# The MLP of the first joint layer as seven products of quarter blocks over 768 tokens, and one block for the compression weights

## The reference

```python
def sq_relu_mlp(h, w1, w2):
    return jnp.square(jax.nn.relu(h @ w1)) @ w2
...
        x = x + ml[5] * sq_relu_mlp(modulate(rms_norm_2(x, norm2_g[i]), ml[3], ml[4]), mlp_w1[i], mlp_w2[i])
        if ctx_later:
            h_ctx = h_ctx + mc[2] * yc
            h_ctx = h_ctx + mc[5] * sq_relu_mlp(modulate(rms_norm_2(h_ctx, norm2_g[i]), mc[3], mc[4]),
                                                mlp_w1[i], mlp_w2[i])
```

## Time and profile before

| | us |
|---|---|
| median of 3 runs | 4087.72 (4080.39 to 4090.18) |
| profiled execution | 4087.81 |
| its span, first to last instruction | 4085.7 |
| PE busy | 3926.6 (96%) |
| DVE busy | 1751.1 (43%) |
| ACT busy | 932.8 (23%) |
| POOL busy | 506.3 (12%) |
| mean granted TensorE clock | 0.978 |

### The profile page before, as it was taken

One profiled execution on the slowest core, in us unless ns is written; L12 is line 12 of the kernel. 1 busy time (PEld: TensorE's weight loads), 2 busy tenths in 40 slices (PEclk: granted clock), 3 DMA queues, 4 the chain that ended last, 5 costly groups with the idle time before them and its releaser, 6 DMA issues.

```text
span 4085.7 us, 42004 instructions
## 1 busy us (share of the span) xinstructions
PE 3926.6 (96%) x16600; PEld 2671.4 (65%) x16604; DVE 1751.1 (43%) x3123; ACT 932.8 (23%) x2131; POOL 506.3 (12%) x414
## 2 busy tenths in 40 slices
PE   9999979999999999999999899999999999999997
PEld 4458436545655565656545578888558888678886
DVE  2654444732673223111010555654675665224343
ACT  1141213621452211100010442020312111212020
POOL 1000000000000000000000421112432121111121
PEclk8999989999999999999999999999999999999999
DMA  3112332021002123223121314443202444112221
GB/s 125 62 42 84 116 98 79 1 74 41 24 1 61 62 82 107 100 99 108 62 72 64 86 30 154 165 167 103 83 21 83 165 165 144 67 62 83 83 83 42
DMA packets 226770, 342.38 MB, mean 84 GB/s; under 512 B 32209, under 2 KB 100209, under 8 KB 226545
## 3 DMA queue, kind: packets, MB, share of 16 engines
q1 hardware_dynamic: 202064, 322.44, 23.0%
q0 software_dynamic: 6816, 10.01, 1.2%
q10 hardware_dynamic: 17696, 7.26, 0.7%
HBM read 334.01 MB, written 4.06 MB: 83 GB/s over the span
## 4 chain that ended last, share of the span: by engine, by line
PE 73%; DVE 3%; POOL 1%; ACT 1%; issue 1%; DMA 0%; DVEq 0%; ACTq 0%; POOLq 0%
PE psum L1638 28%; PE psum L1407 28%; PE psum L1591 5%; PE psum L1595 3%; PE psum L1762 2%; PE psum L1709 2%; PE psum L1739 1%; PE psum L1507 1%; POOL arena L2774 1%; PE psum L1367 1%; DVE small L2594 1%; ACT arena L2079 1%; DVE psum L2590 0%; DVE arena L2609 0%; PE psum L1665 0%
## 5 line engine op out<-in xcount | busy, mean ns | idle before, releaser
L1407 PE MATMUL psum<-H,ring 128*128 128x512 f32 (+1 forms) x3248 | 1160.5, 517 | 38.1 <-DMA ring<-in_cd_in 22.8
L1407 PEld LDWEIGHTS psum<-H,ring 128*128 128x128 f32 x3248 | 622.0, 193 | 554.8 <-issue 483.9
L1638 PE MATMUL psum<-arena,ring 128*128 128x256 f32 x1536 | 342.8, 380 | 2.8 <-ACT arena L1876 2.8
L2296 DVE SCALAR_TENSOR_TENSOR arena<-ring,cond,arena 128x512 f32<-128x512 f32 x448 | 320.5, 754 | 8.0
L1638 PEld LDWEIGHTS psum<-arena,ring 128*128 128x128 f32 x1536 | 290.4, 190 | 44.0 <-ACT arena L1876 5.3
L2731 POOL TENSOR_TENSOR ring<-ring 128x1024 f32<-128x1024 f32 x48 | 159.6, 3325 | 791.0 <-DVE arena L2143 791.0
L1638 PE MATMUL psum<-arena 128*128 128x256 f32 x1152 | 256.3, 379 | 0.4
L1638 PEld LDWEIGHTS psum<-arena 128*128 128x128 f32 x1152 | 218.6, 190 | 30.3 <-ACT arena L1881 0.7
L2594 DVE TENSOR_REDUCE small<-psum 128x1 f32<-128x512 f32 (+7 forms) x352 | 187.0, 566 | 116.8 <-PE psum L1721 51.6
L2279 DVE TENSOR_TENSOR mods<-psum,vec 128x4 f32<-128x4 f32 (+1 forms) x48 | 7.7, 161 | 509.1 <-PE psum L1367 508.2
L1591 PE MATMUL psum<-arena,ring 128*128 128x512 f32 x512 | 225.6, 593 | 0.2 <-issue 0.2
(11 more groups left out here) (230 smaller groups left out, 4612.2 us busy)
## 6 DMA issues: line engine op xcount, KB each, us to landing
ring<-in_mlp_w SPq DMA_DIRECT2D x64, 2048.0 KB, 8.8
ring<-in_ada_w SPq DMA_DIRECT2D x48, 2048.0 KB, 7.9
ring<-in_na_qkv SPq DMA_DIRECT2D x6, 2048.0 KB, 8.0
ring<-in_ab_in SPq DMA_DIRECT2D x5, 2048.0 KB, 8.2
ring<-in_cd_in SPq DMA_DIRECT2D x4, 2048.0 KB, 7.7
ring<-in_pw SPq DMA_DIRECT2D x8, 1024.0 KB, 6.8
ring<-in_at_qkv SPq DMA_DIRECT2D x3, 2048.0 KB, 7.8
ring<-in_ab_out SPq DMA_DIRECT2D x2, 2048.0 KB, 8.2
```

What stands on the lines that cost most here:

```text
L1407: last = nc.tensor.matmul(out, lhs, rhs, start=(k == 0), stop=(k == len(t.pairs) - 1))
L1638: last = nc.tensor.matmul(bank(at, HALF, HALF * m), w[:, i, P * m:P * m + P], x[:, i, :], start=(opens and m == 0 and i == 0), stop=(i == ...
L2296: ins = nc.vector.scalar_tensor_tensor(partial[:, v, :], w[:, k, :], cond[:, k, v:v + 1], partial[:, v, :], ALU.mult, ALU.add)
```

## The change

**The joint MLP** (`joint_mlp` takes the place of `mlp_ctx`) becomes a fast stage. The normed x and context are written side by side into one tensor, `J`, of 8 tiles x 768 columns, which takes the place of `H` and `CH`. The inner layer is made in four quarters of 1024 rows. A quarter is four units up and four down. A unit is seven products, each four matmuls deep over 384 columns, for two output tiles of 128 rows; two units share a 2 MB block of weights, and the ada block rides on the second. There are 32 units on the same 16 weight blocks. Where an output half straddles x and the context, DVE adds it in two parts with the two gates. The steps of `fast_mlp` are parametrised for this (`T`, `hids`, `adds`, `frees`); the other three layers keep their sizes.

**Layer CD**: the two compression weights share one 2 MB block, in four pieces. The group of the block 2048:2464 no longer comes behind a ride, the rides of two groups are gone, and one now rides on the first tile of the block 1536:2048. **AB's out projection** is no longer cut after two tiles where a block rides on it. **at_qkv**: an ada block now rides on its second block.

```diff
+        HC = sb("HC", [P, KD * (S + C)])
+        H = HC[:, 0:KD * S].rearrange("p (t s) -> p t s", s=S)
+        CH = HC[:, KD * S:].rearrange("p (t s) -> p t s", s=C)
+        J = HC[:, :].rearrange("p (t s) -> p t s", s=S + C)
...
-            sums_tile, parts = groups[3][1][2], []
-            for b, tiles, a in groups:
-
-                parts += [(b, tiles[0:2], a), (b, tiles[2:], None)] if a else [(b, tiles, None)]
-            return stage("project", groups=parts, sums_tile=sums_tile, **kw)
+            return stage("project", groups=groups, sums_tile=groups[3][1][2], **kw)
...
-        cd_group(b, tiles, True)
+        cd_group(b, tiles)
...
-        for kv in range(2):
-            b = block(dram["cmp_w1"][kv, 0:CMP_HALF * HD].rearrange("(l d) m -> d l m", d=HD),
-                      dram["cmp_w1"][kv, CMP_HALF * HD:].rearrange("(l d) m -> d l m", d=HD))
-            cmp_freed[b] = (misc_pe, 3 + kv)
-            cd_group(b, [])
...
+        cmp_block = block_of(2 * CMP_HALF * CMP_HID, pieces)
+        cmp_freed[cmp_block] = (misc_pe, 4)
+        cd_group(cmp_block, [])
         b = cd_block(1536, 2048)
         tiles = [t_tile(b, KD, P * j, P, H, S, "act", "silu", Z2[:, 1 + j]) for j in range(4)]
-        cd_group(b, tiles)
+        cd_group(b, tiles[0:1], True)
+        cd_group(b, tiles[1:])
...
+        def joint_mlp(layer):
...
+            normed = norm(sg(1, 0), mod(layer, 3, 0), sq=low_arena, to=(J[:, :, 0:S], J[:, :, S:]),
+                          ctx=(sg(1, 1), mod(layer, 3, 1),
+                               arena[:, 12288:12288 + KD * C].rearrange("p (t s) -> p t s", s=C)))
+            start_ada(layer + 1)
...
+            W, T, k = S + C, (S + C) // 2, KD // 2
...
+            for quarter in range(4):
+                for up in (True, False):
+                    act, t = (J, tu) if up else (hid, [td[0], td[1], hid[:, 0:k, T:W], td[2]])
...
+                    for j in range(2):
...
+                        b = block(view.rearrange("(k p) n -> p k n", p=P))
+                        w = slot(b, KD)
+                        a = next_ada()
+                        for i in range(2):
...
+                            a11, a12, a21, a22 = w[:, 0:k, upper], w[:, k:, upper], w[:, 0:k, lower], w[:, k:, lower]
+                            first = j == 0 and i == 0 and not (up and quarter)
+                            u = dict(id=len(units), b=b, a=a if i else None, k=k, mt=1, up=up, j=j, half=quarter,
+                                     first=first, order=FIRST_ORDER if first else ORDER, t=t, last=False, after={},
...
+                                     pairs={1: (a11, act[:, 0:k, 0:T]), 2: (a12, act[:, k:, 0:T]),
+                                            3: (s4, act[:, k:, T:W]), 4: (a22, t[3]), 5: (s1, t[0]), 6: (s2, t[1]),
+                                            7: (a21, t[2])})
...
+                                u["adds"] = [[[(X[:, m, 0:T], 0, T, mod(layer, 5, 0)(m))],
+                                              [(X[:, m, T:S], 0, S - T, mod(layer, 5, 0)(m)),
+                                               (CX[:, m, :], S - T, T, mod(layer, 5, 1)(m))]] for m in rows]
...
-            at_groups.append((b, tiles, None))
+            at_groups.append((b, tiles, next_ada() if c0 == 512 else None))
...
-        mlp_ctx(0)
+        joint_mlp(0)
...
+                if st["split"] is None:
+                    act.wait_ge(scratch_in, 16 * 16)
...
+                if normed is None:
+                    dve.wait_ge(scratch_in, 16 * 16)
+                    token_sums(st, us[0], (1, 2))
...
+                if "sums_of" in st:
+                    weight_sums(st["sums_of"])
```

More of the change, by code:

```diff
@@ L911, in fast_mlp @@
             tu = [CX[:, 0:4], CX[:, 4:8], CH[:, 0:4], CH[:, 4:8]]
-            st = stage("fast", units=[], sums=sums, tmp=tmp, hid=hid, split=normed)
+            st = stage("fast", units=[], tmp=tmp, split=normed, hids=32)
             t_sets = n_hid = 0
@@ L1538, in compress @@
             def compress(_, v):
-                b1 = cmp_blocks[v]
-                weights(b1)
+                weights(cmp_block)
                 open_bank(6 + v)
                 for l in range(CMP_HALF):
-                    last = nc.tensor.matmul(bank(6 + v, 2 * NCMP), slot(b1, CMP_HALF)[:, l, :],
+                    last = nc.tensor.matmul(bank(6 + v, 2 * NCMP), slot(cmp_block, 2 * CMP_HALF)[:, CMP_HALF * v + l, :],
                                             cmp_in[v][:, 2 * NCMP * l:2 * NCMP * (l + 1)], start=(l == 0),
@@ L2186, in fast, with added @@
                     t1, u2, u3, c, v = (tmp[x][:, 0:cols] for x in ("t1", "u2", "u3", "c", "v"))
-                    def added(dst, src, m, signals):
-                        nc.vector.scalar_tensor_tensor(dst, src, u["gate"][m], dst, ALU.mult, ALU.add).then_inc(signals, 1)
+                    def added(row, col, src, signals):
+                        parts = u["adds"][row][col]
+                        for dst, c0, c1, gate in parts:
+                            ins = nc.vector.scalar_tensor_tensor(dst, src[:, c0:c1], gate, dst, ALU.mult, ALU.add)
+                            if dst is not parts[-1][0]:
+                                step(ins)
+                        ins.then_inc(signals, 1)
                     def c11():
```

135 lines of the change are left out of this document (78 added, 57 removed).

## The result

The changed kernel takes **3994.88 us** in the median of 4 runs (3990.88 to 3999.09). The kernel before, run beside it, takes 4088.95 us (4 runs, 4080.39 to 4091.70). The ratio is 0.9774, with a 95% interval of 0.9761 to 0.9787. The prediction was 3992 us, with a range of 3978 to 4012. The profiled execution has a span of 3989.0 us, where 3990.4 was worked out.

A forecast was written before the change was run, and what follows sets the result against it. PE alone, busy 96% of the span, was taken to bound the kernel. MLP -68.3, layer CD -21.6, AB's out projection -7.5 and at_qkv +2.1 us sum to -95.3, giving 3992 us with a range of 3978 to 4012.

The forecast's parts named there:

- The products: Joint MLP: 896 matmuls of 384 columns at 0.645 us replace 512 of 1.290 us, a gain of 82.6 us.
- The start: MLP start: PE idles 5.6 us for ACT's copy; slow clock adds 2.5 and 2.6; loss 7.7 us net.
- The quarters: Each quarter's first down unit waits 0.6 us for T1's copy before product 2, four times: 2.4 us lost.
- DVE's load: Worst pair of MLP units: DVE needs 31.9 us, PE 37.8, cover 5.9; new vector work costed at nothing.
- The end: After the MLP's last matmul, POOL's six adds of 1.26 us delay PE's sum; with the clock, 4.2 us lost.
- Layer CD: Projection: the 17.98 us wait, its slow tile and one modulation go, the 4.87 us wait stays; 21.6 us gained.
- the term for the slow tile behind the wait: Layer CD: the tile taking 8.81 instead of 7.0 us speeds up once the wait goes, 1.8 us gained.
- at_qkv: The added ride costs one modulation ahead of the attention and DVE's addition: +2.1 us.
- The vector side: Rival, chance 0.14: DVE and POOL fall behind in the MLP units, costing 8 to 25 us: 4000 to 4017 us.
- The CD wait: Rival, chance 0.06: layer CD's wait moves and stays, so 19.8 us are not gained: 4012 us.
- The matmul's cost: Rival, chance 0.01: a 384-column MLP matmul costs what a 512-column one does, 191 us more: 4183 us.
- The gain beyond the forecast: Rival, chance 0.03: PE's waits at both ends of the MLP vanish, 3978 us.

The follow-up runs named there:

- the second run: The kernel before with only the edits in layer CD, AB's out projection and at_qkv, the MLP left as it was: 4066.78 us, ratio 0.9944.
- either edit alone: The kernel before with only the compression weights merged, or only the rides of layer CD and at_qkv moved: spans 4069.3 and 4071.9 us.
- the two mends: Changed kernel with ACT's early first-product copy, POOL's five squares before its last sum, and POOL's first weight sum waiting for T2: span 3988.4 us.
- the first mend: Changed kernel, with ACT copying the first unit's first product before the context's norm tiles: span 3985.3 us, joint stage 621.16 us.
- the last kernel: The changed kernel with the two mends, and one layer CD ride moved from the block 2048:2464 to the group of ukv: 3980.51 us, ratio 0.9740.

## Why the prediction was right, point by point

**What bounds the kernel.** PE alone, as read. With one more DVE instruction of 1.75 us per unit it waited for DVE nowhere in the units, with three it did.

**The products.** The middle between the 256-column and the 512-column pace, 0.645 us, is what the trace shows, 2.58 us for four. From first to last matmul the stage takes 608.4 us, where the terms gave 681.5 - 72.5 = 609.0.

**The start.** The wait was 5.87 us (5.6 forecast), with the cause named. Its clock terms came out differently in each run. In the first profile, 1332.74 to 1347.11 is 14.4 us for two products worth 5.2, so 9.2 lost against 3.0 before: 6.2. In the second it is 15.4 us, and 0.45 in the next row, so 7.7, the forecast. Reading a gap as its whole cost would have been wrong: without it only 2.8 us came back.

**The quarters** were right to 0.1 us in all in the idle time, but idle time is not the whole price. The last record of product 1 and the first of product 2 begin 1.07 us apart (1570.70 and 1571.77), where the pace is 0.32, and the next one comes 0.1 late. That is some 0.85 us a quarter and 3.4 in all, not 2.4, and offsets 1.0 of the 1.5 us by which the start was cheaper in the first profile. **DVE's load** was nothing on the path in the units, as costed. The worst pair came to about 29 us and not 31.9, but the cover of a pair was the wrong measure: the slack ahead of the modulation, 0.2 us in the working (18.6 and 18.8) and 1.8 measured, is what the load experiments ran into.

**The end** was mis-sized: 5.6 and not 4.2 us. POOL's chain ran 8.45 us and not 7.6, because its adds begin 1.4 us apart and not 1.26, and it began 0.5 us before the last matmul's end and not 0.8. DVE's last adds, stretched beside it, and the last row's square end before POOL does. The run with POOL's adds ahead shows that POOL's chain is the cause.

**Layer CD** was forecast at 21.6 us. The projection, which is what the forecast priced, gave 15.7 in the first profile; with the attention behind it 21.0, and that agreement is luck. Right are the wait of 17.98 us, the modulation, and the wait that stays. The step that failed is the term for the slow tile behind the wait (1.8 us), with the idea that the low clock goes with the gap: the tile takes 8.81 us with no wait ahead of it, and before it stands only a modulation of 16 one-column matmul records with 0.93 us of idle time. Nor does that modulation decide it. Behind the same rows the tile takes 7.11 us in the changed kernel's second profile; of the ten profiles without the wait four have the slow tile and six don't. Two more places ran at the low clock in the first profile and not in that of the kernel before: 4.5 in place of 2.9 us from 447.14 on, and 12.2 in place of 8.9 from 604.91 on. From the modulation at 410 us (417 before) to the projection's last, the nine profiles with both edits and the ride in its old place take 220.1 to 223.6 us, against 239.2 before. So the projection gains 15.7 to 19.1 us and never the 21.6; what decides where the low clock falls stays open. What hid the miss is a stretch that nobody edited, the attention of layer CD. Busy time there, in the kernel before:

```profile
656.60:879.60 223.00, 211.72 (x1249) 115.67 (x1250) 125.91 (x416) 109.74 (x364) 8.16 (x6) 0.94 0.11 39
```

In the changed kernel, its first profile:

```profile
634.00:851.70 217.70, 206.34 (x1250) 112.30 (x1250) 125.70 (x416) 109.50 (x364) 8.15 (x6) 0.97 0.11 40
```

And in its second profile:

```profile
630.00:856.00 226.00, 214.70 (x1251) 117.70 (x1252) 125.82 (x416) 109.77 (x364) 8.15 (x6) 0.93 0.11 38
```

The same instructions take 217.4 to 225.9 us in the 14 profiles, by the granted clock (0.97 to 0.93). The first profile pair holds 5.3 us of that in favour of the change, and the two slow places in the projection count 4.9 us against it; neither is a merit or a fault of the edits that these runs can show. This stretch and the next are also most of what the second run (the other edits alone) lacked: there the attention took 223.3 us, 5.7 more than in the changed kernel, and the next one, spread to spread around at_qkv, 471.7 against 467.4; the kernel's start took 2.2 us more, and the projection 3.5 less. The medians, which lie 94.1 us apart, are the better measure; the interval of their ratio makes it 87 to 98 us.

**at_qkv** was given +2.1 us, and the stretch around it shows -1.3. In the changed kernel's first profile the norm's spread ran at full clock (1.12 us, against 2.08 before). From that spread to the MLP norm's it takes 467.8 us before, and 467.6 and 468.5 in the two other profiles without the moved ride. In the three runs with the moved ride in which both spreads ran at the low clock, as before, it takes 470.3, 470.4 and 471.7: 1.8 to 4.1 us more, where the first profile of the changed kernel has 467.4. But the spreads are no sure sign of the clock between them: one profile with both at full clock (the load run with one instruction) takes 471.2, and the mean of all eleven with the moved ride is 469.2, against 468.0 of the three without. These runs neither confirm nor exclude the forecast's 2.1, since the clock can hide it whole.

**The rivals.** The vector side did not fall behind. The CD wait did not move, but either edit alone would have left 4 us of it. The matmul's cost goes with its columns. The gain beyond the forecast, which was given 0.03, is what the two mends and the moved ride then brought, in a kernel of its own.

## What to carry to other kernels

Seven products for eight save what they promise if the sums fit under the matmuls with a deadline each, not only in total: write down, for every step on the helping engine, when PE asks for it. Price a gap of PE by what would bind once it is gone, here 2.8 of 5.9 us. Where blocks go through a ring of slots, the wait for one is decided three blocks earlier, and two edits that look independent may only work together.

## What the runs showed of the hardware that I had not expected

The low clock does not need a long gap, nor does a gap always bring it. The tile behind a modulation in layer CD takes 8.81 us in one profile of the changed kernel and 7.11 in the other, each time with 0.93 us of idle time before the modulation and none behind it. With the first mend, PE idled 3.54 us before product 5 and went on at nearly full pace (5.56 us for two products); in the last kernel it idled 3.46 us at the same place and took 8.10. One profile is therefore no measure of a change of 5 us in this kernel, while a stretch without such places repeats to 0.3 us (the old MLP stage: 691.98, 691.81, 691.75, 691.71). The Trainium skill (TensorE: Matmul & The Clock Gate, section HAM oscillation) lays the low clock to gaps, behind which each restart begins cold. The two waits of 3.5 us in the load experiment agree with that; the slow tile behind the modulation and the restart of 5.56 us don't. What else decides it no run here shows.

An overlap of DVE and POOL does not vanish when one of them is moved, it goes to the next DVE instruction with two SBUF inputs: from S4 to the residual adds, and from T2 to T4.
